# The two latent projections as one group of eight half-bank tiles, with x in five pieces

## The chip, the cores and the metric

The kernel runs on one core of a Trainium2 chip. The metric is the device time of one execution, in microseconds (us). The engines are TensorE (PE: matmuls, turned tiles), ScalarE (ACT), VectorE (DVE), GpSimd (POOL) and SyncE (SP, which issues most transfers); each runs its own instructions in order and waits for the others at semaphores.

## The reference, cut to what matters

A block of 256 tokens of width 2048 goes through two layers. The change touches only the start of the first: the normed x times the first 1024 columns of `w_in`, which are the query latent `q_a` and the key and value latent `c_kv`, 512 columns each, and what reads them.

```python
h = _rmsnorm(x, pre_norm_g)
proj = jnp.einsum('bsd,de->bse', h, w_in)
(q_a, c_kv, k_rope, z_mla, ...) = jnp.split(proj, cuts, axis=-1)
q = jnp.einsum('bsr,re->bse', _rmsnorm(q_a, q_a_norm_g), w_q_b)
kv = jnp.einsum('bsr,re->bse', _rmsnorm(c_kv, kv_a_norm_g), w_kv_b)
```

## The kernel before

**Units.** Every weight matrix is cut into units of 128 x 1024 fp32 values (512 KB). A unit is loaded by SP into one of four slots (`w_raw`), rounded by ACT into `w_hi`, and the rest `w_raw - w_hi` is made by DVE as `w_lo`, both in one of three slots. In this text the two halves of the split of unit i together are called W(i). A projection product is three matmuls: hi by hi, hi by the operand's lo, lo by hi. The helper `run` goes through a phase's units; before unit i it makes sure that splits up to i + 2 are in the plan, and after it adds split i + 3. So ACT's half of W(i + 3) waits until PE has used unit i. `plan_work` writes one list of steps, and each engine takes its part of every step in that order; nothing else sets the order.

**The start.** ACT issues the identity and x (four pieces of 512 KB, `first_loads`); SP issues the first unit, the constants, three more units and some small rows. x comes with tokens on the partitions. `x_tile(k)` turns one tile of 128 columns of both token halves: two transposes on PE into one of three side banks, a copy to SBUF on DVE (`x_T`, L1881), gain and rounding on ACT (`op_hi`, L1576), a square on ACT (L1581), and the square's sum on POOL (L2393). The lo half of tile k - 1 (`op_lo`, L1886) follows on DVE. Six tiles are turned ahead of the first unit and ten later, one in two PE tiles.

**The latents.** Phases `qa` and `kva` each hold one group of four tiles of 128 output columns, over 16 tiles of x: 8 units of 2 x 512, a unit being 24 matmuls. Call the 16 units of both u0 to u15. Phase `kr` (2 units, u16 and u17, of 24 matmuls each) and phase `q` (16 units of 18 matmuls) follow. When a group is done, DVE multiplies each tile by the factor R of the first norm (`latent`, L1976), ACT squares it (L1609), POOL adds, and 4 PE tiles later `latent_split` makes the operand's halves: ACT (L1616), DVE (L1990).

**Factors.** A norm's factor is made by `row_sum` (PE sums the squares, DVE L1897, POOL's power, DVE L1903) and `row_spread` (PE), then copied by DVE (L1911). `factor` jobs, and the job `vectors`, stand in `pending`, and `pump` runs one step of each active job after a unit. `vectors` turns the small rows (`cols`, after u6), converts the positions (`pos_f`, DVE L1917), multiplies them out on PE (`angle`, after u7, which waits for `pos_f`), and makes the sines in DVE steps (L1923 to L1952). R is `r1`, the latent factors are `rq` and `rkv`.

Of the kernel before, what the change touches and what calls it, by code (L numbers as in the profile page):

```python
# [12 lines left out]
ALU = mybir.AluOpType  # L13
# [12 lines left out]
H1, DN, RD, DV, LORA = 16, 128, 64, 128, 512  # L26
C_QA, C_KV, C_KR = 0, LORA, 2 * LORA
# [181 lines left out]
FOUR, THREE, ONE = ("f0", "f1", "f2", "f3"), ("f0", "f1", "f2"), ("f0",)  # L209
KV = ("f0", "f2", "t0", "t1")  # L210
TOKENS = ("t0", "t1")


def groups_of(c0, n, cols=512, tiles=FOUR):
    return [(c0 + g * cols, cols, tiles) for g in range(n)]


def phases():
    ph = {}

    def put(name, *args, **kw):
        ph[name] = Phase(name, *args, **kw)

    put("qa", "w_in", groups_of(C_QA, 1), KT, "h", S)
    put("kva", "w_in", groups_of(C_KV, 1), KT, "h", S)
    put("kr", "w_in", [(C_KR, P, ONE)], KT, "h", S)
# [40 lines left out]
def plan_work(sem):  # L267
# [39 lines left out]
    def later(step, tiles=4):  # L307
        deferred.append([tiles, step])
# [10 lines left out]
    def run(p, evac):  # L319
        out = {}  # L320
        for i in range(p.first, p.end):
            split_to(i + LEAD)
            u = units[i]
            for m, tile in enumerate(u.tiles):
                if u.k0 == 0:
                    out[m] = banks.take()
                last = m == len(u.tiles) - 1
                s = add("tile", i, m, bank=out[m], marks="proj" if u.last else "used" if last else "")
                if last:
                    plan.used[i] = s["proj" if u.last else "used"]  # L330
                for d in deferred:
                    d[0] -= 1
                for d in [d for d in deferred if d[0] <= 0]:
                    deferred.remove(d)
                    d[1]()
                if u.last:
                    out[m].ends(evac(u.g, m, out[m].slot, s["proj"]))
            if not (p.hold and i == p.end - 1):
                split_to(i + N_SPLIT)
            if (i - p.first) % p.period == p.period - 1:  # L340
                pump()
# [41 lines left out]

    add("first_loads", dma="ld_ident ld_x0 ld_x1 ld_x2 ld_x3")
    zero = add("zero_rows", marks="rows_zero")["rows_zero"]
    pre = add("load_pre", dma="ld_pre", zero=zero)["ld_pre"]
    load()
    done["con"] = add("load_con", dma="ld_con")["ld_con"]
    for _ in range(N_RAW - 1):
        load()  # L390
# [25 lines left out]
    for k in range(KT):  # L416
        if k < 6:
            x_tile(k)
        else:
            later(lambda k=k: x_tile(k), 2 * (k - 5))  # L420
        if k in (2, 4):
            split()
# [42 lines left out]

    def latent(which):
        def evac(g, m, pb, got):
            sc = scratch.take() if m else None
            s = add("latent", which, m, marks="evac sq" + (" sq_acc" if m else ""), pb=pb, got=got, scratch=sc)
            if m:  # L470
                sc.ends(s["sq_acc"])

            def split_latent():
                done["lat_" + which, m] = add("latent_split", which, m, marks="op_hi op_lo", x=s["evac"])["op_lo"]
            later(split_latent)
            if m == 3:
                pending.append(factor("r" + which, [s["sq_acc"]], delay=4))
            return s["evac"]
        return evac

# [90 lines left out]

    run(ph["qa"], latent("q"))
    run(ph["kva"], latent("kv"))
    run(ph["kr"], evac_kr)
    flush()
# [439 lines left out]
class Memory:  # L1015
# [221 lines left out]
def tensor_engine(nc, m, plan, S_):  # L1237
# [16 lines left out]
    def tile(s):  # L1254
# [10 lines left out]
        for k in range(u.nk):  # L1265
            kt = u.k0 + k
            operand_ready(u.phase.operand, kt)
            x_hi, x_lo = m.operand(u.phase.operand, kt)
            first, last = kt == 0, kt == u.phase.ktiles - 1
            if kind == "f":  # L1270
# [25 lines left out]
    def x_tile(s):  # L1296
        k, = s.args
        bank = s.of["bank"]
        pe.wait_ge(S_("ld_ident"), 16)
        pe.wait_ge(S_(f"ld_x{k // 4}"), 16)  # L1300
        pe.wait_ge(*bank.after)
        b = m.side[bank.slot]
        turn(b[:, 0:P], m.x_in[:, 0, COLS(k)], ident)
        turn(b[:, P:S], m.x_in[:, 1, COLS(k)], ident).then_inc(S_("xt_t"), 1)
# [246 lines left out]
def scalar_engine(nc, m, a, plan, S_):  # L1551
# [301 lines left out]
def vector_engine(nc, m, plan, S_):  # L1853
# [707 lines left out]
```

## Time and profile before

| | us |
|---|---|
| median of 3 runs | 2036.23 |
| lowest, highest | 2033.36, 2036.35 |
| the profiled execution | 2034.77 |
| its span | 2033.5 |

The 1.3 us between the profiled time and its span lie outside the instructions. The profiled execution is 1.5 us under the median. Times in the rows are us from the start of the span, the second number being the duration, and a bracket at the end says how long the engine was idle before and who released it.

### The profile page before, as it was taken

How to read it: one execution, taken by the hardware profiler on the slowest of the kernel's cores; microseconds unless marked ns; L12 is line 12 of the kernel's file. 1: busy time of each engine (PE TensorE's matmuls, PEld its weight loads, DVE VectorE, ACT ScalarE, POOL GpSimd, SP SyncE). 2: the span in 40 equal slices, each digit the busy share in tenths (PEclk: the TensorE clock that was granted, in tenths of full speed). 3: DMA queues.
4: the chain of work that ended last, by engine and by line, in shares of the span. 5: the costliest groups of instructions: out<-in, count | busy, mean ns of one | idle time of the engine just before them, and what ended most of it. 6: DMA issues, size and time to landing. Idle time of an engine off the chain costs nothing.

```text
span 2033.5 us, 37130 instructions
## 1 busy us (share of the span) xinstructions
PE 1978.8 (97%) x15778; PEld 1941.9 (95%) x15778; DVE 1169.5 (58%) x1736; ACT 875.5 (43%) x1264; POOL 298.9 (15%) x336
## 2 busy tenths in 40 slices
PE   7999999999999999999999799999999998999999
PEld 6999999999999999999999699999999998999987
DVE  5765665555554545644554655576467676564654
ACT  5444454434444434444444433445443333344443
POOL 2110010202010003300211521030011122030200
PEclk9999999999999999999999899999999999999999
DMA  7466555556666565565565364443564443556564
GB/s 241 138 193 173 152 154 157 156 177 183 182 185 181 184 186 176 180 192 182 185 221 182 126 192 137 145 136 113 157 177 135 125 125 115 177 180 192 186 226 158
DMA packets 177695, 343.79 MB, mean 169 GB/s; under 512 B 10478, under 2 KB 19050, under 8 KB 177002
## 3 DMA queue, kind: packets, MB, share of 16 engines
q1 hardware_dynamic: 176154, 337.16, 54.8%
q10 hardware_dynamic: 1376, 4.26, 0.6%
q8 instruction: 124, 2.03, 0.4%
q14 instruction: 41, 0.34, 0.0%
HBM read 335.09 MB, written 6.29 MB: 168 GB/s over the span
## 4 chain that ended last, share of the span: by engine, by line
PE 82%; issue 8%; DVE 3%; POOL 2%; ACT 1%; POOLq 0%; DVEq 0%; ACTq 0%
PE bank L1245 81%; DVE w_lo L1866 1%; POOL arena L2467 1%; ACT w_hi L1567 1%; POOL scratch L2464 1%; DVE arena L2146 0%; POOL arena L2511 0%; POOL stats L2413 0%; DVE head_factor L1903 0%; DVE arena L2249 0%; DVE best L2247 0%; ACT scratch L1725 0%; DVE ob_lo L2151 0%; ACT ob_hi L1723 0%; POOL acc_a L2393 0%
## 5 line engine op out<-in xcount | busy, mean ns | idle before, releaser
L1866 DVE TENSOR_TENSOR w_lo<-w_raw,w_hi 128x1024 fp32r<-128x1024 f32 (+2 forms) x644 | 784.9, 1222 | 786.4 <-ACT w_hi L1567 785.1
L1567 ACT ACTIVATE w_hi<-w_raw 128x1024 fp32r<-128x1024 f32 (+2 forms) x644 | 661.5, 1031 | 925.0 <-PE bank L1245 924.5
L1245 PE MATMUL bank<-hb_hi,w_hi 128*128 128x256 f32 x2448 | 700.3, 286 | 0.1
L1245 PE MATMUL bank<-hb_lo,w_hi 128*128 128x256 f32 x2448 | 694.1, 284 | 0.0
L1245 PE MATMUL bank<-hb_hi,w_lo 128*128 128x256 f32 x2448 | 694.1, 284 | 0.0
L1245 PE MATMUL bank<-ob_hi,w_hi 128*128 128x256 f32 (+1 forms) x2224 | 650.9, 293 | 9.1 <-DVE ob_lo L2151 6.6
L1245 PE MATMUL bank<-ob_hi,w_lo 128*128 128x256 f32 (+1 forms) x2224 | 631.7, 284 | 0.0
L1245 PE MATMUL bank<-ob_lo,w_hi 128*128 128x256 f32 (+1 forms) x2224 | 630.5, 284 | 0.0
L1245 PEld LDWEIGHTS bank<-hb_hi,w_hi 128*128 128x128 f32 x2448 | 470.4, 192 | 2.4 <-DVE w_lo L1866 1.3
L1245 PEld LDWEIGHTS bank<-hb_lo,w_hi 128*128 128x128 f32 x2448 | 470.5, 192 | 0.4
L1245 PEld LDWEIGHTS bank<-hb_hi,w_lo 128*128 128x128 f32 x2448 | 470.5, 192 | 0.0
L1245 PEld LDWEIGHTS bank<-ob_hi,w_hi 128*128 128x128 f32 x2224 | 424.8, 191 | 13.8 <-issue 4.4
L1245 PEld LDWEIGHTS bank<-ob_lo,w_hi 128*128 128x128 f32 x2224 | 424.7, 191 | 1.5
L1245 PEld LDWEIGHTS bank<-ob_hi,w_lo 128*128 128x128 f32 x2224 | 424.0, 191 | 0.0
L1245 PE MATMUL bank<-arena 128*128 128x64 f32 (+4 forms) x618 | 102.6, 303 | 10.4 <-DVE arena L2333 3.0
L1245 PEld LDWEIGHTS bank<-arena 128*128 128x128 f32 x618 | 80.6, 191 | 14.0 <-DVE arena L2333 3.3
L2474 POOL TENSOR_TENSOR arena<-scratch,arena 128x256 f32<-128x256 f32 x32 | 31.9, 1030 | 278.7 <-DVE scratch L1976 278.7
L1245 PE MATMUL bank<-w_hi,ob_hi 128*128 128x512 f32 (+1 forms) x192 | 69.0, 359 | 0.0
L1245 PE MATMUL bank<-w_lo,ob_hi 128*128 128x512 f32 (+1 forms) x192 | 68.5, 357 | 0.0
L1245 PE MATMUL bank<-w_hi,ob_lo 128*128 128x512 f32 (+1 forms) x192 | 68.4, 356 | 0.0
L2447 POOL TENSOR_TENSOR arena<-arena,factor 128x256 f32<-128x256 f32 x16 | 15.3, 990 | 276.5 <-DVE arena L1976 276.5
L2464 POOL TENSOR_TENSOR scratch<-scratch,head_factor 128x256 f32<-128x256 f32 x16 | 13.3, 833 | 242.9 <-ACT head_factor L1680 242.9
(252 smaller groups left out, 1227.4 us busy)
## 6 DMA issues: line engine op xcount, KB each, us to landing
w_raw<-in_w_in SPq DMA_DIRECT2D x436, 512.0 KB, 3.7
w_raw<-in_w_out SPq DMA_DIRECT2D x64, 512.0 KB, 4.1
w_raw<-in_w_o_conv SPq DMA_DIRECT2D x32, 512.0 KB, 4.4
w_raw<-in_w_o_mla SPq DMA_DIRECT2D x32, 512.0 KB, 3.8
w_raw<-in_w_branch SPq DMA_DIRECT2D x32, 512.0 KB, 4.0
w_raw<-in_w_kv_b SPq DMA_DIRECT2D x16, 512.0 KB, 3.9
w_raw<-in_w_q_b SPq DMA_DIRECT2D x16, 384.0 KB, 3.2
arena<-x_kept SPq DMA_DIRECT2D x2, 2048.0 KB, 9.1
```

Of the source, the lines that this page charges most:

```text
L1245: return nc.tensor.matmul(dst, lhsT, rhs, start=start, stop=stop, skip_group_check=True)
L1567: act(dst, src, ACT.Copy).then_inc(S_("w_hi"), 1)
L1866: tt(low, src, high.bitcast(F32), ALU.subtract).then_inc(S_("w_lo"), 1)
L2447: tt(m.u_t[:, t, :], m.u_t[:, t, :], m.R, ALU.mult).then_inc(S_("conv_b"), 1)
L2464: tt(z, z, ring[s.of["head"].slot][:, 0:S], ALU.mult).then_inc(S_("silu"), 1)
L2467: tt(y, z, y, ALU.mult).then_inc(S_("gated"), 1)
L2474: tt(y, m.scratch[s.of["scratch"].slot][:, 0:S], y, ALU.add).then_inc(S_("merged"), 1)
```

## The change

Phases `qa` and `kva` become one phase `lat` with a group of eight tiles over 1024 columns. A unit is then one tile of x by 1024 columns, 4 KB rows where they were 2 KB, and still 24 matmuls; there are still 16. Two tiles share a PSUM bank: the odd one starts without the start flag and is placed in the upper 256 columns, and both are read out after the odd one's last matmul. x comes as 2, 2, 4, 4 and 4 tiles. SP issues a second unit ahead of the constants. Four tiles are turned ahead of the first unit and twelve later, one in six PE tiles. The latent splits come 2 tiles after their read-out, not 4, and the job `rq` waits 2 pumps, not 4.

```diff
-    put("qa", "w_in", groups_of(C_QA, 1), KT, "h", S)
-    put("kva", "w_in", groups_of(C_KV, 1), KT, "h", S)
+    put("lat", "w_in", groups_of(C_QA, 1, 2 * LORA, EIGHT), KT, "h", S)
...
-        out = {}
+        out, two = {}, len(p.groups[0][2]) > 4
...
-                    out[m] = banks.take()
+                    out[m] = out[m - 1] if two and m % 2 else banks.take()
...
-                if u.last:
+                if u.last and not two:
+                    out[m].ends(evac(u.g, m, out[m].slot, s["proj"]))
+                elif u.last and m % 2:
+                    evac(u.g, m - 1, out[m].slot, s["proj"])
                     out[m].ends(evac(u.g, m, out[m].slot, s["proj"]))
...
-    add("first_loads", dma="ld_ident ld_x0 ld_x1 ld_x2 ld_x3")
+    add("first_loads", dma="ld_ident ld_x0 ld_x1 ld_x2 ld_x3 ld_x4")
...
     load()
+    load()
     done["con"] = add("load_con", dma="ld_con")["ld_con"]
-    for _ in range(N_RAW - 1):
+    for _ in range(N_RAW - 2):
         load()
...
-        if k < 6:
+        if k < 4:
             x_tile(k)
         else:
-            later(lambda k=k: x_tile(k), 2 * (k - 5))
-        if k in (2, 4):
+            later(lambda k=k: x_tile(k), 6 * (k - 3))
+        if k in (0, 2):
             split()
...
+        later(split_latent, 2)
+        if m == 3:
+            pending.append(factor("r" + which, [s["sq_acc"]], delay=2 if which == "q" else 4))
...
-    run(ph["qa"], latent("q"))
-    run(ph["kva"], latent("kv"))
+    run(ph["lat"], latent)
...
+X_PARTS = ((0, 2), (2, 4), (4, 8), (8, 12), (12, 16))
...
+        if len(u.tiles) > 4:
+            return self.proj[bank][:, S * (m % 2):S * (m % 2) + S]
...
-            first, last = kt == 0, kt == u.phase.ktiles - 1
+            first, last = kt == 0 and not (len(u.tiles) > 4 and t % 2), kt == u.phase.ktiles - 1
```

**Order, place A.** DVE around the conversion of the positions (`small`, the CAST), between u6 and u8. In the kernel before, where no turned tile is left:

```order
L1866 TENSOR_TENSOR w_lo<-w_raw,w_hi 128x1024 [waits w_hi] x2
L1897 TENSOR_SCALAR stats0<-bank7 128x2 [waits rf_sum]
L1903 TENSOR_SCALAR acc_b<-con,stats0 128x128 [waits rf_pow]
L1903 TENSOR_SCALAR acc_b<-con,stats0 128x128
L1866 TENSOR_TENSOR w_lo<-w_raw,w_hi 128x1024 [waits w_hi]
L1915 COPY cols<-bank5 128x112 [waits cols_t]
L1917 CAST small<-arena 1x256 [waits ld_pos]
```

and in the changed kernel, whose line numbers are 5 higher here, from W(8) on:

```order
L1871 TENSOR_TENSOR w_lo<-w_raw,w_hi 128x1024 [waits w_hi]
L1886 COPY arena<-bank6 128x256 [waits xt_t]
L1891 SCALAR_TENSOR_TENSOR hb_lo<-arena,cols,hb_hi 128x256 [waits op_hi]
L1871 TENSOR_TENSOR w_lo<-w_raw,w_hi 128x1024 [waits w_hi]
L1920 COPY cols<-bank7 128x112 [waits cols_t]
L1922 CAST small<-arena 1x256 [waits ld_pos]
L1886 COPY arena<-bank5 128x256 [waits xt_t]
L1891 SCALAR_TENSOR_TENSOR hb_lo<-arena,cols,hb_hi 128x256 [waits op_hi]
```

The CAST stands right behind W(9) in both, but now turned tile 12 and eleven others have gone through DVE and ACT between the splits ahead of it, and the work on R comes after it.

**Order, place B.** PE at the end of u7, the kernel before:

```order
L1245 MATMUL bank3<-hb_hi,w_hi 128x256
L1245 MATMUL bank3<-hb_lo,w_hi 128x256
L1245 MATMUL bank3<-hb_hi,w_lo 128x256
L1245 MATMUL bank7<-small,con 128x256 [waits rf_mean,pos_f]
L1245 MATMUL bank4<-hb_hi,w_hi 128x256 [waits w_lo]
```

and the changed kernel:

```order
L1250 MATMUL bank3<-hb_hi,w_hi 128x256
L1250 MATMUL bank3<-hb_lo,w_hi 128x256
L1250 MATMUL bank3<-hb_hi,w_lo 128x256
L1250 MATMUL bank6<-small,con 128x256 [waits x_T,pos_f]
L1250 MATMUL bank0<-hb_hi,w_hi 128x256 [waits op_lo,w_lo]
```

The matmul on `small` (`angle`) keeps its place behind u7 and its wait for the CAST of place A.

**Order, place C.** DVE at the end of the latents (L1976, now L1992: the read-out; L1990, now L1998: the split's lo half). Before:

```order
L1866 TENSOR_TENSOR w_lo<-w_raw,w_hi 128x1024 [waits w_hi]
L1957 TENSOR_TENSOR small2<-cols 128x8 [waits cols]
L1959 TENSOR_TENSOR small2<-cols,small2 128x8 [waits dve_own]
L1960 TENSOR_TENSOR small2<-cols,small2 128x8
L1976 TENSOR_TENSOR arena<-bank4,factor 128x256 [waits proj]
L1976 TENSOR_TENSOR arena<-bank0,factor 128x256 [waits proj]
L1976 TENSOR_TENSOR arena<-bank1,factor 128x256 [waits proj]
L1976 TENSOR_TENSOR arena<-bank2,factor 128x256 [waits proj]
L1866 TENSOR_TENSOR w_lo<-w_raw,w_hi 128x2x256 [waits w_hi]
```

and now:

```order
L1992 TENSOR_TENSOR arena<-bank0,factor 128x256 [waits rf_out,proj]
L1992 TENSOR_TENSOR arena<-bank0,factor 128x256
L1998 SCALAR_TENSOR_TENSOR ob_lo<-arena,cols,ob_hi 128x256 [waits op_hi] x2
L1992 TENSOR_TENSOR arena<-bank1,factor 128x256 [waits proj]
L1992 TENSOR_TENSOR arena<-bank1,factor 128x256
L1998 SCALAR_TENSOR_TENSOR ob_lo<-arena,cols,ob_hi 128x256 [waits op_hi] x2
L1992 TENSOR_TENSOR arena<-bank2,factor 128x256 [waits proj]
L1992 TENSOR_TENSOR arena<-bank2,factor 128x256
L1998 SCALAR_TENSOR_TENSOR ob_lo<-arena,cols,ob_hi 128x256 [waits op_hi] x2
L1992 TENSOR_TENSOR arena<-bank3,factor 128x256 [waits proj]
L1992 TENSOR_TENSOR arena<-bank3,factor 128x256
L1871 TENSOR_TENSOR w_lo<-w_raw,w_hi 128x2x256 [waits w_hi]
```

The first split of phase `q`, W(18), stood behind four read-outs and now stands behind eight, with three pairs of latent splits between them. From the second unit of the third query group on, the instructions of every engine stand as before.

## Rows read from the trace of the kernel before

**Rows 1.** The page: busy time by engine, share of the span, instructions.
```profile
PE 1978.8 (97%) x15778; PEld 1941.9 (95%) x15778; DVE 1169.5 (58%) x1736; ACT 875.5 (43%) x1264; POOL 298.9 (15%) x336
```

**Rows 2.** Waits of PE, 0 to 110 us: total, times, longest in us.
```profile
PE bank L1303 <- DMA arena<-in_x: 5.8, 2, 3.0
PE bank L1245 <- POOL acc_b L2393: 3.5, 1, 3.5
...
PE bank L1245 <- DVE acc_b L1903: 1.4, 1, 1.4
...
PE bank L1245 <- DVE acc_a L1903: 1.2, 1, 1.2
```

**Rows 3.** Timeline, PE's first projection matmul: start, duration, engine, line, tiles.
```profile
11.92 0.58 PE L1245 MATMUL bank<-hb_hi,w_hi 128*128 128x256 f32 x1
```

**Rows 4.** The load tile w_raw, issues at 2.4 and 3.2 us: time until landed.
```profile
L1185 SPq DMA_DIRECT2D w_raw<-in_w_in x2: 542/656/769, 2.4 to 3.2; - x2
...
DMA to landing us min/median/max: 10.5/11.5/12.5
```

**Rows 5.** Timeline of ACT, 13 to 34 us: the w_hi halves of four units.
```profile
13.68 1.04 ACT L1567 ACTIVATE w_hi<-w_raw 128x1024 fp32r<-128x1024 f32 x1
...
17.07 1.05 ACT L1567 ACTIVATE w_hi<-w_raw 128x1024 fp32r<-128x1024 f32 x1
...
29.48 1.04 ACT L1567 ACTIVATE w_hi<-w_raw 128x1024 fp32r<-128x1024 f32 x1
...
33.59 1.05 ACT L1567 ACTIVATE w_hi<-w_raw 128x1024 fp32r<-128x1024 f32 x1
```

**Rows 6.** Timeline of DVE, 30 to 34 us: the w_lo half of a unit.
```profile
30.55 1.23 DVE L1866 TENSOR_TENSOR w_lo<-w_raw,w_hi 128x1024 fp32r<-128x1024 f32 x1 [1.44 <-ACT w_hi L1567]
```

**Rows 7.** Stretches: busy us and records by engine, granted clock, DMA share, GB/s.
```profile
41.00:43.00 2.00, 2.00 (x12) 2.00 (x11) 0.70 (x4) 0.00 (x0) 0.71 (x1) 0.50 0.93 393
43.00:45.00 2.00, 2.00 (x14) 2.00 (x14) 0.03 (x1) 1.06 (x1) 0.00 (x0) 0.71 0.90 300
120.00:150.00 30.00, 30.00 (x254) 29.94 (x253) 17.96 (x26) 14.44 (x19) 2.22 (x3) 1.00 0.65 191
1129.00:1143.00 14.00, 7.90 (x35) 7.29 (x35) 11.12 (x17) 5.32 (x13) 10.86 (x13) 0.52 0.15 61
```

**Rows 8.** Timeline of all engines, 62 to 65 us: the factor of the query latent.
```profile
62.66 0.15 DVE L1897 TENSOR_SCALAR stats<-bank 128x2 f32<-128x2 f32 x1
...
64.26 0.68 PE L1245 MATMUL bank<-acc_a,con 128*128 128x128 f32 x4 [1.17 <-DVE acc_a L1903]
```

**Rows 9.** Timeline of DVE, 45 to 100 us.
```profile
46.30 0.27 DVE L1917 CAST small<-arena 1x256 f32<-1x256 int32 x1
...
51.40 1.76 DVE L1990 SCALAR_TENSOR_TENSOR ob_lo<-arena,cols,ob_hi 128x256 fp32r<-128x256 f32 x4
...
65.43 0.42 DVE L1939 SCALAR_TENSOR_TENSOR rope<-scratch 128x256 f32<-128x256 f32 x1
...
66.68 0.42 DVE L1911 COPY factor<-bank 128x256 f32<-128x256 f32 x1
...
73.70 1.41 DVE L1976 TENSOR_TENSOR arena<-bank,factor 128x256 f32<-128x256 f32 x4
...
81.31 1.01 DVE L1866 TENSOR_TENSOR w_lo<-w_raw,w_hi 128x512 fp32r<-128x512 f32 x2
```

**Rows 10.** Timeline of ACT, 45 to 100 us.
```profile
49.73 1.69 ACT L1616 ACTIVATE ob_hi<-arena,cols 128x256 fp32r<-128x256 f32 x4
...
71.13 1.04 ACT L1567 ACTIVATE w_hi<-w_raw 128x1024 fp32r<-128x1024 f32 x1
```

**Rows 11.** Timeline of PE: the angle matmul, the meta turns, the rope of query group 0.
```profile
47.39 0.69 PE L1245 MATMUL bank<-small,con 1*128 1x256 f32 x2
...
79.27 1.17 PE L1352 MATMUL bank<-con,arena 16*128 16x16 f32 x16
...
94.97 0.59 PE L1245 MATMUL bank<-arena,con 128*128 128x256 f32 x2
```

More of the change, by code:

```diff
@@ L210 @@
 KV = ("f0", "f2", "t0", "t1")
+EIGHT = tuple(f"f{j}" for j in range(8))
 TOKENS = ("t0", "t1")
@@ L462, in plan_work, with latent, split_latent @@
     pending.append(vectors())
[L466 to L479, printed above, removed]
+    def latent(g, n, pb, got):
+        which, m = ("q", "kv")[n // 4], n % 4
+        sc = scratch.take() if m else None
+        s = add("latent", which, m, marks="evac sq" + (" sq_acc" if m else ""), pb=pb, got=got, scratch=sc)
+        if m:
+            sc.ends(s["sq_acc"])
+        def split_latent():
+            done["lat_" + which, m] = add("latent_split", which, m, marks="op_hi op_lo", x=s["evac"])["op_lo"]
+        later(split_latent, 2)
+        if m == 3:
+            pending.append(factor("r" + which, [s["sq_acc"]], delay=2 if which == "q" else 4))
+        return s["evac"]
     def clear_halves(kind, free):
@@ L1299, in x_tile @@
         pe.wait_ge(S_("ld_ident"), 16)
-        pe.wait_ge(S_(f"ld_x{k // 4}"), 16)
+        pe.wait_ge(S_(f"ld_x{[k < hi for lo, hi in X_PARTS].index(True)}"), 16)
         pe.wait_ge(*bank.after)
@@ L1556, in first_loads @@
         nc.scalar.dma_start(m.con[:, 0:P], a["const_f"][:, 0:P]).then_inc(S_("ld_ident"), 16)
-        for j in range(4):
-            x = a["x"][0, :, j * 512:(j + 1) * 512].rearrange("(b p) n -> p b n", p=P)
-            nc.scalar.dma_start(m.x_in[:, :, j * 512:(j + 1) * 512], x).then_inc(S_(f"ld_x{j}"), 16)
+        for j, (lo, hi) in enumerate(X_PARTS):
+            x = a["x"][0, :, lo * P:hi * P].rearrange("(b p) n -> p b n", p=P)
+            nc.scalar.dma_start(m.x_in[:, :, lo * P:hi * P], x).then_inc(S_(f"ld_x{j}"), 16)
     def split(s):
@@ L1983, in latent @@
         which, t = s.args
-        out_by(s, m.LAT[:, 4 * (which == "kv") + t, :], m.R, done["r1"])
+        at = S * (t % 2)
+        ve.wait_ge(*s.of["got"])
+        ve.wait_ge(*done["r1"])
+        tt(m.LAT[:, 4 * (which == "kv") + t, :], m.proj[s.of["pb"]][:, at:at + S], m.R, ALU.mult).then_inc(S_("evac"), 1)
     def latent_split(s):
```

## The prediction

> **What bounds the kernel now.** I read the page first: PE is busy 97% of the span [rows 1], so only PE's idle time and its clock can be won or lost. Then PE's waits up to 110 us [rows 2]: 5.8 us for x to land, one wait of 3.5 for the sum of x's squares (`acc_b`) and one of 1.2 and one of 1.4 for a latent's factor. The reader is to see that these are few and single, and that the matmuls begin at 11.92 [rows 3]. Then the laps of ACT and DVE [rows 5, 6], because the splits W(i) and the turned tiles hand each other on between these two: ACT's half of a split, DVE's half 1.07 us behind it (30.55 less 29.48), DVE's copy of a turned tile, ACT's rounding and square of it, ACT's next half. With one turned tile between two splits a lap is 17.07 - 13.68 = 3.39 us, with two 33.59 - 29.48 = 4.11. PE's unit takes 24 x 0.118 = 2.83 (30.00 us by 254 records [rows 7]) and 0.2 per turned tile. In this stretch ACT and DVE bound the kernel, not PE. Last the clock: after the wait of 3.5 us the granted clock is 0.50, the 1.2 GHz level, from 41 to 43 and 0.71 on average from 43 to 45 [rows 7], which costs 1.0 + 0.6 = 1.6 us of matmul time.
>
> **The start.** W(0) no longer waits for turned tiles 1 and 2, and x's first two tiles come as 256 KB. DVE's half of W(0) should end about 1 us before 11.92. I cost it at nothing, because what comes below is set by the laps and not by PE: even from 11.92, eight units with the slow clock at the beginning (8 x 2.83, some 2.5, my estimate, for the slow matmuls, 10 turned tiles at 0.2) bring PE to the end of u7 at 39.1 or so.
>
> **Place A and B, the wait for `pos_f`.** PE's `angle` behind u7 waits for the CAST behind W(9). W(2) can't start before its load has landed. It is the third unit issued in both kernels, behind the same bytes: 3.2 + 12.5 = 15.7 [rows 4]. From W(2) to W(9) there are seven laps, five with one turned tile (4, 5, 8, 9, 12) and two with two (6 and 7, 10 and 11): 5 x 3.39 + 2 x 4.11 = 25.2. So ACT's half of W(9) starts at 41.0, DVE's at 42.0, and with its 1.23 [rows 6] and the copy and CAST of 0.27 each [rows 9] `pos_f` is there at 43.7. PE waits there from about 39.3: a new wait of 4.4 us. Queued behind it on PE are u8, whose W(8) is ready at 39.9, and everything else. In the kernel before `angle` ran at 47.39 [rows 11], so PE passes this point 3.6 us earlier than before, but with work left that it had then done: turned tiles 14 and 15 (0.4), the row sum and the row spread of `r1` (1.0). Lead: 3.6 - 1.4 = 2.2.
>
> The load's price has a second value. The rows of a load are now 4 KB and not 2. The Trainium skill, page "DMA: Bandwidth & Descriptors", section "Why small descriptors are slow (HBM only)", states about 3 cycles per packet beside one per 32 bytes; as an estimate from that page, 67 against 65.5 cycles per 2 KB, W(2) would land 0.3 us earlier and the sum would be 0.3 less. No row here shows a 4 KB load.
>
> **The clock behind that wait.** The wait of 3.5 cost 1.6 in slow matmuls [rows 2, 7]; this one is longer, so I take the same 1.6. Lead: 0.6. Bounds: 0, if the engine's idle time falls otherwise than before, and 3.2, two such stretches.
>
> **The wait for R.** The row sum of `r1` stood behind u5, its spread behind u6, and only two splits stood ahead of it on DVE. Now the sum comes after u9 and the spread after u10, and DVE has ahead of it, from the end of u9: ACT's and DVE's halves of W(12), which wait for u9 (1.07 + 1.15), the three sine steps L1939 to L1943 (66.68 - 65.43 = 1.25 [rows 9]) and then 64.26 - 62.66 = 1.6 from DVE's first step of a factor to PE's spread [rows 8]. That is 5.1, against u10 and the row sum, 3.3: a wait of 1.8 to 2.0. I take 2.0, since W(12) also queues behind two steps of `turns`. The 3.5 us wait for `acc_b` goes: between turned tile 15 and the sum lies all of u9. Its saving is already in the 3.6 above. Lead: 0.6 - 2.0 = -1.4, a lag.
>
> **The factor of the query latent.** `rq`'s sum (0.5), wait (1.2 [rows 2]) and spread (0.5) stood between u11 and u13 and now stand behind `kr`. So u15 ends 2.2 - 1.4 = 0.8 us earlier than before.
>
> **Place C, the read-out.** Before, half of the latents was read out in the middle, under `kva`. Now all eight come behind u15. DVE's first read-out follows ACT's half of W(17) by 73.70 - 71.13 = 2.57 [rows 9, 10]; that half starts when u14 is used, which is u15 and `kr` (3 x 2.83) ahead of 79.27, 70.7, and 69.8 now. So the read-out starts at 72.4. A pair is a lap of its own: two read-outs (1.41 / 4 = 0.35 each [rows 9]), two squares on ACT as long, two hi halves (1.69 / 4 = 0.42 [rows 10]), the second lo half (1.76 / 4 = 0.44 [rows 9]). The pair after it waits for that: 0.7 + 0.35 + 0.85 + 0.44 and the handing over, 2.4 us. Three laps bring the last pair to 79.6. Its squares end at 80.7; behind them ACT and DVE do W(18), two pieces, 1.7 us (DVE's two take 1.01 [rows 9], ACT's first lies ahead of them). W(18) is ready at 82.4. PE has done `kr` and the meta turns at 79.6 (79.27 + 1.17 [rows 11], 0.8 earlier) and the row sum of `rq` at 80.1. A wait of 2.3, where there was none.
>
> Then the spread of `rq`, one unit of 2.1 later. DVE has ahead of it W(19) 0.95, the bounds' small steps 0.6, two lo halves 0.9, two memsets 0.6, `kr`'s read-out 0.3, W(20) 0.95, and 1.6 as above: 5.9. A wait of 3.7. Of these the 0.6 and 0.6 are estimates from neighbouring short rows; bounds of the whole are 2.5 and 4.5. The wait for `rkv` falls from 1.4 [rows 2] to about 0.4, since the splits wait less when PE is late.
>
> Up to the rope of query group 0's successor at 94.97 [rows 11], behind which every engine's order is as before: -0.8 + 1.0 (sum and spread of `rq`) + 2.3 + 3.7 + 0.4 - 1.4 = +5.2 us.
>
> **The clock behind those waits.** PE then stands idle for 6 of 8.2 us. The nearest case is 1129 to 1143, where the clock was 0.52 on average over 14 us with PE busy 7.9 [rows 7], which cost up to 3.9. Here one stretch costs 1.6 and a run as there 3.9; I take 1.9, nearer to the first, as the idle time is shorter. Sum: +5.2 + 1.9 = +7.1 us.
>
> The sum stands on the profiled execution, 2034.8, and gives 2041.9 there. The profiled execution is 1.5 under the median, and nothing in the change touches that distance: 2036.2 + 7.1 = 2043.3.
>
> **The rivals.**
> Late waits hidden: the 8 us of `kr`, meta turns and row sum cover the read-out laps, if a pair takes under 1.4 us because ACT and DVE work at two pairs at once. For it: ACT and DVE are only half busy over the span [rows 1]. Against it: both run in order and the order has the lo halves of a pair ahead of the next read-out. It takes away 2.3 + 3.7 + 1.9 and leaves the `rkv` wait at 1.4: 2043.3 - 6.9 = 2036.4. Chance 0.14.
> Early wait missing: `pos_f` comes before PE is through with u7, and only the late waits hold. PE then goes on at W(8) and W(9), u9 starts at 43.4 and not at 48.5 (43.8, u8 with two turned tiles 3.2, slow clock 1.6): 2043.3 - 5.1 = 2038.2. It would take W(2) landed 4 us earlier. Chance 0.11.
> The other side: handing over between ACT and DVE gets cheap when less is turned per unit. Its place is both laps; it decides where a lap with one turned tile falls to PE's own 3.0 us and a pair of read-outs to 1.4. Both cases above then hold together: 2043.3 - 6.9 - 5.1 = 2031.3, faster. Against it stands the lap of 3.39 that the trace has with just one turned tile [rows 5]. Chance 0.12.
> A further 3 us of slow clock at the three waits, to 2047 or so, is within the forecast.
>
> **How the numbers follow.** A measurement of this kernel can tell about 0.2% from no change, 4.1 us: faster is under 2032.2, slower over 2040.3. The forecast with its bounds spans 2040.3 to 2049 and has a chance of 0.63. The two middle rivals are within 0.2%: 0.25. The other side is 0.12. A range from 2034.5 to 2049 leaves out the other side and some 0.05 of the tails.
>
> **What would show it.** In the profile of the changed kernel: PE's first projection matmul near 10.8; a PE wait of about 4.4 us for DVE's CAST ending near 43.7, with the granted clock at 0.50 behind it; a PE wait of about 2 for `acc_b` on DVE near 57, and none on POOL; DVE's read-outs in four pairs, 2.4 us apart, from 72.4; PE waits of 2.3 for `w_lo` and 3.7 for `acc_a` between 80 and 89. The forecast is wrong if the first is under 1 us, which would mean that the laps are not what holds W(9), or if the pairs of read-outs stand closer than 1.5 us.

## The result, and the profile after

The changed kernel takes 2042.2 us (median of 6 runs, 2041.2 to 2043.4) against 2035.7 for the kernel before beside it: a ratio of 1.0035, 95% interval 1.0023 to 1.0046. A second batch of the same kernel gave 2043.1 and 1.0037 (1.0025 to 1.0050). It is slower, within the range and 1.1 us under the forecast of 2043.3. The profiled execution took 2042.17, its span 2040.9. The agreement hides an error in one term of the forecast, the slow clock, which the second half of this section takes apart.

The busy row answers to [rows 1]:

```profile
PE 1977.9 (97%) x15778; PEld 1940.0 (95%) x15778; DVE 1170.1 (57%) x1736; ACT 875.8 (43%) x1264; POOL 299.0 (15%) x336
```

PE's share is the same 97%, with 0.9 us less busy time in a span that is 7.4 longer. Its waits from 0 to 110 us answer to [rows 2] (total, times, longest):

```profile
PE bank L1250 <- DVE w_lo L1871: 4.6, 2, 4.2
...
PE bank L1250 <- DVE small L1922: 4.0, 1, 4.0
...
PE bank L1250 <- DVE acc_b L1908: 2.6, 2, 1.9
PE bank L1250 <- DVE acc_a L1908: 1.9, 1, 1.9
```

POOL's 3.5 for `acc_b` is gone and four waits stand in its place. The timeline of PE shows where each of them ends (start, duration, then in brackets the idle time and who ended it); the first row answers to [rows 3] and the last, the rope of query group 0's successor, to 94.97 in [rows 11]:

```profile
10.76 0.55 PE L1250 MATMUL bank<-hb_hi,w_hi 128*128 128x256 f32 x1 [0.96 <-DVE hb_lo L1891]
...
43.09 1.22 PE L1250 MATMUL bank<-small,con 1*128 1x256 f32 x2 [4.02 <-DVE small L1922]
...
57.60 0.68 PE L1250 MATMUL bank<-acc_b,con 128*128 128x128 f32 x4 [1.89 <-DVE acc_b L1908]
...
85.77 0.58 PE L1250 MATMUL bank<-ob_hi,w_hi 128*128 128x256 f32 x1 [4.22 <-DVE w_lo L1871]
...
91.51 0.68 PE L1250 MATMUL bank<-acc_a,con 128*128 128x128 f32 x4 [1.88 <-DVE acc_a L1908]
...
105.32 0.59 PE L1250 MATMUL bank<-arena,con 128*128 128x256 f32 x2
```

They are 4.0, 1.9, 4.2 and 1.9 us, and a fifth of 0.7 ends at 102.65. The last row stands 10.35 us behind the kernel before. I call this point Z. From here on all engines run the same instructions in the same order in both kernels. DVE's side of the four waits, which answers to [rows 6, 9]:

```profile
41.44 1.23 DVE L1871 TENSOR_TENSOR w_lo<-w_raw,w_hi 128x1024 fp32r<-128x1024 f32 x1 [1.44 <-ACT w_hi L1572]
...
42.76 0.27 DVE L1922 CAST small<-arena 1x256 f32<-1x256 int32 x1
...
54.74 0.42 DVE L1944 SCALAR_TENSOR_TENSOR rope<-scratch 128x256 f32<-128x256 f32 x1
...
74.28 0.75 DVE L1992 TENSOR_TENSOR arena<-bank,factor 128x256 f32<-128x256 f32 x2
...
76.91 0.74 DVE L1992 TENSOR_TENSOR arena<-bank,factor 128x256 f32<-128x256 f32 x2
...
79.81 0.74 DVE L1992 TENSOR_TENSOR arena<-bank,factor 128x256 f32<-128x256 f32 x2
...
82.41 0.74 DVE L1992 TENSOR_TENSOR arena<-bank,factor 128x256 f32<-128x256 f32 x2
84.15 2.16 DVE L1871 TENSOR_TENSOR w_lo<-w_raw,w_hi 128x512 fp32r<-128x512 f32 x3 [1.00 <-ACT w_hi L1572]
```

W(9) and, right behind it, the CAST; the three sine steps from 54.74 ahead of r1's diag; the read-outs in pairs 2.6, 2.9 and 2.6 us apart, and W(18) only then. The stretches of TensorE's clock (columns as in [rows 7]: busy time of PE, its weight loads, DVE, ACT, POOL, then the granted clock):

```profile
13.00:95.00 82.00, 69.19 (x514) 67.07 (x513) 51.85 (x107) 39.72 (x72) 16.15 (x21) 0.88 0.52 166
41.30:48.10 6.80, 5.01 (x20) 4.36 (x21) 4.67 (x9) 2.68 (x6) 0.76 (x2) 0.50 0.42 133
58.40:61.80 3.40, 3.40 (x18) 3.40 (x18) 0.72 (x3) 0.42 (x1) 0.00 (x0) 0.50 0.98 283
82.30:89.10 6.80, 3.33 (x15) 3.34 (x16) 5.53 (x17) 4.29 (x11) 1.94 (x2) 0.50 0.33 101
92.50:95.90 3.40, 3.40 (x16) 3.22 (x15) 2.27 (x6) 0.00 (x0) 0.00 (x0) 0.50 0.39 128
```

Before Z the clock is at 0.50, the 1.2 GHz level, in four stretches, 20.4 us together, where the kernel before has one of 3.4 (40.8 to 44.2). As an estimate I count half of PE's busy time in such a stretch as lost: (5.01 + 3.40 + 3.33 + 3.40) / 2 = 7.6 us, against 1.7.

**What becomes of the 10.35.** I matched DVE's arithmetic instructions of the two traces one by one from the end. The lag stays between 10.35 and 10.56 up to 1601 us (times as in the kernel before), is 9.07 at 1605, stays near 9 up to 1684, is 7.41 at 1688 and stays there. Set side by side, the same two time spans of before and of after show what the falls are (columns as above):

```profile
1600.00:1605.00 5.00, 5.00 (x32) 5.00 (x31) 1.94 (x4) 0.57 (x1) 0.00 (x0) 0.66 0.58 187
1682.00:1687.00 5.00, 5.00 (x31) 5.00 (x32) 2.88 (x6) 0.00 (x1) 0.00 (x0) 0.66 0.33 108
```

```profile
1600.00:1605.00 5.00, 5.00 (x45) 5.00 (x44) 4.21 (x10) 1.06 (x1) 0.74 (x1) 1.00 0.48 132
1682.00:1687.00 5.00, 5.00 (x45) 5.00 (x44) 3.79 (x6) 1.06 (x1) 0.85 (x1) 1.00 0.30 105
```

The execution of before has a half-clock stretch of 3.4 us in each, where the mean falls to 0.66; that of after has none. (A third, at 1631 in before, costs nothing, since the lag is 9.05 on both sides of it.) In the second batch of the changed kernel, with the same instructions, they are back:

```profile
1607.00:1612.00 5.00, 5.00 (x32) 5.00 (x31) 1.78 (x4) 0.73 (x1) 0.00 (x0) 0.66 0.53 175
1689.00:1694.00 5.00, 5.00 (x33) 5.00 (x31) 2.72 (x6) 0.17 (x1) 0.00 (x0) 0.66 0.34 108
```

There the lag is 7.93 at Z, its start having been 1.15 us earlier, and 6.85 at the end, with no step at these two places. So each profiled execution holds a few stretches of slow clock by chance, and about 3 of the 10.35 came back by such a chance. The two steps, 1.5 and 1.7 us, also say how good the estimate by halves is: it gives 1.7 for each, and 1.7 for the third, which cost nothing. It's an upper one.

### The profile page after: what moved, and what is told of

The parts are those of the page before. It is cut to its first block, busy times and chain, and to the rows that moved or that the text cites. A ratio compares the mean times of both kernels' runs of the same rounds, so it can differ in the third digit from the quotient of the medians.

```text
span 2040.9 us, 37138 instructions
## 1 busy us (share of the span) xinstructions
PE 1977.9 (97%) x15778; PEld 1940.0 (95%) x15778; DVE 1170.1 (57%) x1736; ACT 875.8 (43%) x1264; POOL 299.0 (15%) x336
## 4 chain that ended last, share of the span: by engine, by line
PE 82%; issue 9%; DVE 5%; ACT 2%; POOL 2%; DMA 0%; ACTq 0%; POOLq 0%; DVEq 0%
PE bank L1250 81%; DVE w_lo L1871 2%; ACT w_hi L1572 1%; POOL arena L2475 1%; POOL scratch L2472 1%; DVE arena L2154 0%; POOL stats L2421 0%; POOL arena L2519 0%; ACT scratch L1586 0%; DMA arena<-in_x 0%; DVE ob_lo L1998 0%; DVE head_factor L1908 0%; DVE arena L1886 0%; DVE arena L2257 0%; ACT hb_hi L1581 0%
```

## The experiments

To read all of them in one way I split the time up to Z into three parts: the start of the first projection matmul; PE's idle time behind it (the sum of its waits of over 0.2 us); and half of PE's busy time in half-clock stretches, as an estimate of what the clock took. Where the three are subtracted from those of before, Z follows within 1.4 us, mostly within 0.6. Batches compare each kernel with the kernel before on the same chip (medians 2035.2 to 2035.7). The ratio isn't the quotient of the two medians: in the batch of experiments 1 to 4, for one, 7 of 30 runs of the kernel before took only 2029 to 2030.4 us. The four columns up to Z are those of one profiled execution, which isn't always a typical one: it took 2037.8 in experiment 1 and 2040.3 in 6, 2.2 and 4.1 under the median, and 2037.5 in 7, 3.8 over it; in the others it lies within 1.6.

| kernel | first matmul | idle | clock | Z | median | ratio (95%) |
|---|---|---|---|---|---|---|
| before | 11.92 | 7.3 | 1.7 | 94.97 | 2035.7 | |
| changed | 10.76 | 13.5 | 7.6 | 105.32 | 2042.2 | 1.0035 (1.0023 to 1.0046) |
| changed, again | 9.61 | 13.0 | 6.4 | 102.90 | 2043.1 | 1.0037 (1.0025 to 1.0050) |
| 1 CAST early | 9.66 | 13.2 | 1.8 | 99.00 | 2040.0 | 1.0028 (1.0017 to 1.0039) |
| 2 r1 first | 10.15 | 12.0 | 6.5 | 102.47 | 2041.2 | 1.0036 (1.0023 to 1.0048) |
| 3 read-outs in a row | 10.54 | 9.3 | 5.6 | 99.22 | 2038.6 | 1.0024 (1.0013 to 1.0034) |
| 4 all three | 9.70 | 5.6 | 4.6 | 94.68 | 2032.3 | 0.9992 (0.9982 to 1.0002) |
| 5 start alone | 9.61 | 8.1 | 3.2 | 94.87 | 2034.6 | 0.9993 (0.9984 to 1.0002) |
| 6 grouping alone | 12.73 | 13.2 | 5.3 | 104.88 | 2044.4 | 1.0039 (1.0027 to 1.0051) |
| 7 five edits | 11.26 | 7.5 | 5.0 | 97.76 | 2033.7 | 0.9993 (0.9983 to 1.0002) |
| 8 tiles 8 apart | 9.78 | 8.2 | 3.4 | 95.84 | 2035.1 | 0.9999 (0.9990 to 1.0008) |
| 9 later row sum | 10.38 | 7.9 | 1.7 | 95.21 | 2034.0 | 0.9994 (0.9985 to 1.0003) |
| 10 both | 11.29 | 7.6 | 1.6 | 95.90 | 2033.7 | 0.9991 (0.9982 to 1.0000) |
| 11 later spread | 11.23 | 6.1 | 0 | 92.15 | 2029.0 | 0.9973 (0.9963 to 0.9982) |

**Experiment 1: the CAST early.**

```diff
     def vectors():
+        done["pos_f"] = add("pos_cast", marks="pos_f")["pos_f"]
         for _ in range(5):
             yield
...
-        s = add("cols", marks="cols_t cols pos_f", bank=b)
+        s = add("cols", marks="cols_t cols", bank=b)
...
+
+    def pos_cast(s):
         ve.wait_ge(*done["pos"])
         v.tensor_copy(m.pos_f, m.pos_i).then_inc(S_("pos_f"), 1)
```

> Edit: DVE's CAST of the positions (pos_f) stands behind W(1) instead of behind W(9), nothing else. My theory (laps of ACT and DVE): the early PE wait of 4.0 us at 39 to 43 goes, because PE's angle step no longer waits for W(9). But the laps themselves don't get faster: W(9) is still ready at 42.6, W(10) near 46, W(11) near 50, then W(12) and the three sine steps, so DVE's diag of r1 comes near 54.7 and not 57.4, and PE, there since about 49.5, waits for it 4.5 to 5.5 us instead of 1.9. Of the 4.0 only 2.8 are kept: 2042.2 - 2.8 = 2039.4 us, between 2037.5 and 2041 with one half-clock stretch of 1.7 more or less. Rival in the record (the early wait missing is worth 5.1): 2037.1. Rival that the order of DVE has nothing to do with it, and PE waits for splits anyway: the wait at 39 stays over 3 us under w_lo's name and the time at 2042.

Measured: 2040.0, near the expected 2039.4. The CAST runs at 23.06, directly behind W(4) and not behind W(1) as I had it; that is still 15.8 us ahead of its use. The timeline of PE:

```profile
38.84 0.67 PE L1251 MATMUL bank<-small,con 1*128 1x256 f32 x2 [0.69 <-DVE arena L1887]
...
41.99 0.33 PE L1309 MATMUL bank<-con,arena 128*128 128x128 f32 x1 [1.58 <-DVE cols L1921]
...
48.78 0.58 PE L1251 MATMUL bank<-con,acc_b 128*128 128x1 f32 x4 [1.11 <-POOL acc_b L2404]
...
54.34 0.68 PE L1251 MATMUL bank<-acc_b,con 128*128 128x128 f32 x4 [2.01 <-DVE acc_b L1909]
```

The 4.0 us wait for the CAST has become 0.7 at the same `angle` matmul, so DVE's order is its cause. R's spread comes at 54.34 (54.7 expected), so the laps held back most of what was won. The size of that I had right and the shape wrong: the remaining idle time is not one wait of 5 us but three single ones, of 1.6 for the copy of `cols` (behind W(9) on DVE as the CAST was, and it holds the bank of the next turned tile), 1.1 and 2.0. Idle time thus fell by only 0.4. What fell in this execution is the clock's part, 7.6 to 1.8; the runs of this kernel go from 2034.5 to 2042.5, so that isn't shown for a typical one.

**Experiment 2: r1's first steps ahead of the sine steps.**

```diff
-            pending.appendleft(factor("r1", [done["x_sq"]], delay=1))
+            active.insert(0, factor("r1", [done["x_sq"]], delay=1))
```

> Edit: DVE's first two steps of r1's factor (mean, diag) stand ahead of the three sine steps instead of behind them, nothing else. My theory: the wait of 1.9 us for R's spread at 55.7 shrinks by the 1.25 us of the three sine steps to 0.6 or 0.7, the other waits stay (4.0 early, 4.2 + 1.9 + 0.7 late). 2042.2 - 1.2 = 2041.0 us; 2039.3 if the half-clock stretch of 58.4 to 61.8 behind that wait goes too (its cost is 3.4 / 2 = 1.7). Rival (the wait is made by W(12), which needs u9, and not by the sine steps): the wait stays at 1.9 and the time at 2042.2.

```profile
56.27 0.68 PE L1250 MATMUL bank<-acc_b,con 128*128 128x128 f32 x4 [0.63 <-DVE acc_b L1908]
```

The wait is 0.63 and not 1.89: the three sine steps of DVE are its cause, as the prediction had it, and the half-clock stretch at 58.4 is gone too. No new wait has come, and Z comes 2.85 us earlier. Of that 0.6 is an earlier start. The median is 1.0 under that of the changed kernel (1.9 under its second batch), but the two intervals overlap nearly wholly: the wait is shown, a gain in time is not.

**Experiment 3: the read-outs in a row.**

```diff
-        later(split_latent, 2)
+        later(split_latent, 8)
```

> Edit: the splits of the latents are put off by 8 tiles instead of 2, so the eight read-outs on DVE and the eight squares on ACT stand in a row, then W(18) and W(19), then the hi and lo halves of the latents. My theory (pairs hand over between ACT and DVE and hold W(18) back): read-outs 0.35 apart from 74.3 to 77.1, W(18) ready near 79.5 instead of 85.6, so PE's wait of 4.2 for w_lo goes, and that of 1.9 for acc_a falls to 0.5 to 1: 6.8 becomes about 1.2. With it go the half-clock stretches at 82.3 to 89.1 and 92.5 to 95.9 in part (5.1 us if both went, half of that taken). 2042.2 - 5.6 - 2.5 = 2034.1 us, between 2031.5 and 2037. Early waits stay 4.0 and 1.9. Rival (the wait there is the price of eight tiles at once and not of their order): w_lo's wait stays above 3 us and the time at 2041 to 2042.

Timeline of DVE, then of PE:

```profile
74.00 2.74 DVE L1992 TENSOR_TENSOR arena<-bank,factor 128x256 f32<-128x256 f32 x8
...
82.46 0.55 PE L1250 MATMUL bank<-ob_hi,w_hi 128*128 128x256 f32 x1 [1.20 <-DVE ob_lo L1998]
```

The eight read-outs take 2.74 us in a row, and PE's wait for W(18) is gone; it now waits 1.2 for a latent's lo half, and the one of 1.9 for `acc_a` is gone. The late waits are 2.5 and not 6.8 (1.2 expected). So the order of the pairs makes most of the late waits, and not the number of eight tiles. The time is 2038.6, short of 2034.1 by 1.3 in idle time and by the clock, of which only 2.0 came back, and by stretches behind Z.

**Experiment 4: the three together.** The diff is that of the three.

> Edit: the three edits together (CAST behind W(1), r1's first steps ahead of the sine steps, the latents' splits put off by 8 tiles). My theory: the wait for the CAST gone, the wait for R's spread ending near 53.5 instead of 57.6 (2.8 + 1.2 = 4.0 us kept), the late waits about 1.2 instead of 6.8 (5.6), clock 2.5: 2042.2 - 4.0 - 5.6 - 2.5 = 2030.1 us, between 2027 and 2033, so faster than the kernel before (2035.7) as well. Rival (the grouping costs what it costs, whatever the order): not below 2038.

Measured: 2032.3, inside the expected range; Z is 10.6 us earlier than in the changed kernel. Singly the three edits took 2.2, 1.0 and 3.6 us off the median, together 9.9, which is more than their sum; in idle time it is 0.4, 1.6 and 4.3 against 7.9. The loss of the change is thus made by three places in the order and not by the half banks or the 4 KB loads, which this version keeps; its ratio (0.9992) is that of the start alone with two groups (0.9993, experiment 5). Against the kernel before, the interval reaches to 1.0002, so it isn't shown to be faster. This kernel and that of experiment 1 have the same two waits, 0.7 and 1.6, between 38 and 43 us. The same stretch of each, first experiment 1, then experiment 4:

```profile
38.00:49.00 11.00, 7.62 (x59) 6.80 (x57) 7.31 (x15) 6.44 (x12) 3.00 (x4) 1.00 0.55 176
```

```profile
38.00:49.00 11.00, 8.74 (x47) 8.04 (x46) 7.09 (x14) 5.86 (x11) 2.84 (x4) 0.69 0.54 173
```

In one of them the clock stays at 1.00, in the other it falls, for 6.8 us from 41.1 on. Waits of this size don't set the clock by themselves.

**Experiments 5 and 6: the two halves of the change alone.** The start on the kernel before (two groups stay):

```diff
-        if k < 6:
+        if k < 4:
             x_tile(k)
         else:
-            later(lambda k=k: x_tile(k), 2 * (k - 5))
-        if k in (2, 4):
+            later(lambda k=k: x_tile(k), max(k - 3, 2 * (k - 5)))
+        if k in (0, 2):
```

> The kernel before with the start of the change alone: x in five pieces, w_raw's second load ahead of con's, four tiles turned ahead and W(0) and W(1) behind turned tiles 0 and 2; two groups of four tiles stay, and turned tile 15 stays where it is in the kernel before (20 tiles in), since R has to be there for the first read-out behind u7. My theory: the first projection matmul comes near 10.8 instead of 11.9, W(2) starts near 16.2 instead of 17.1, and the wait for acc_b behind turned tile 15 stays at 3 to 3.5 us, so the start gives back 0.9 to 1.1 us and no wait is added: 2035.2 - 1.0 = 2034.2 us, between 2033 and 2036. Rival (the start carries part of the loss, through the loads or through fewer tiles ahead): over 2037.

and the grouping with the start of before:

```diff
-        if k < 4:
+        if k < 6:
             x_tile(k)
         else:
-            later(lambda k=k: x_tile(k), 6 * (k - 3))
-        if k in (0, 2):
+            later(lambda k=k: x_tile(k), 6 * (k - 5))
+        if k in (2, 4):
```

> The changed kernel with the grouping alone: eight tiles of one group two to a bank, but x in four pieces, con's load behind the first w_raw load, six tiles turned ahead, the rest six tiles of the projection apart (turned tile 15 at 60 tiles, 12 earlier). My theory: W(2) starts at 17.1, so W(9) and the CAST end 0.9 to 1.8 us later (44 to 45) and PE waits there 4 to 5 us; R's factor is 1.5 units earlier, ahead of the sine steps, and its wait of 1.9 falls under 0.7, perhaps with its half-clock stretch (1.7); the late waits stay 4.2 + 1.9 + 0.7. Changed kernel 2042.2 + 1.4 - 1.7 - 0.8 = 2041.1 us, between 2039.5 and 2043: the whole loss comes with the grouping. Rival (the loss comes from the start, not from the grouping): 2035 to 2037.

The start alone: 2034.6, as expected a small gain or none (its interval holds 1). The first matmul comes 2.3 us earlier and Z only 0.1: a new wait of 1.5 for a turned tile, and 1.5 more of the clock around the same 3.47 for `acc_b`. The grouping alone: 2044.4 (5 runs, 2040.3 to 2045.5), the whole loss and more. I missed by 3.3; the profiled execution was one of the two at 2040.3, so its rows explain a part only: the first matmul came at 12.73, and R's wait fell only to 1.5, since its diag on DVE, now ahead of the sine steps, still stands behind W(11), which waits for u8 and so for PE's own wait for the CAST. So the three places of experiment 4 come with the grouping, which puts the read-outs of eight tiles behind one unit and the turned tiles between the splits for longer.

**Experiments 7 to 11: is there a version that beats both?** Seven has the edits of four, `cols` in the middle of a unit and the latents' splits after 7 tiles; eight has turned tiles 8 apart as well. Nine is seven with r1's row sum one unit later and the latents' splits after 8 tiles again, ten is the same with turned tiles 8 apart.

```diff
+        later(cols, 4)
...
-        later(split_latent, 8)
+        later(split_latent, 7)
```

> The three edits of before together, and two more: DVE's copy of cols stands in the middle of a unit, ahead of a split and not behind W(9), and the latents' splits are put off by 7 tiles, so that those of the first pair stand ahead of W(19). Three-edit version 2032.3. My theory: the wait of 1.6 at 40.4 for cols goes, but what follows is bound by the laps to W(11) and W(12), so R's spread still ends near 54 and at most 0.3 us are kept in idle time; the late wait of 1.2 for a latent's lo half falls to about 0.5. 2032.3 - 1.0 = 2031.3 us, and 2028 if the half-clock stretch of 41.1 to 47.9 (6.8 us, 3.4 lost at most) is gone as well; between 2027.5 and 2032. Rival (each PE wait counts by itself): 2032.3 - 1.6 - 0.7 = 2030.0 without the clock, with R's spread near 52.7.

```diff
-            later(lambda k=k: x_tile(k), 6 * (k - 3))
+            later(lambda k=k: x_tile(k), 8 * (k - 3))
...
-        b, ang, turns = side.take(), scratch.take(), scratch.take()
+        b, ang, turns = side.take(), heads.take(), heads.take()
```

> As the version with five edits, and the turned tiles stand 8 tiles of the projection apart and not 6, one to each unit (the angle's buffers are two head_factor tiles instead of two scratch tiles, so that the longer row of turned tiles doesn't run into them). My theory: every lap of ACT and DVE then has one turned tile and takes 3.39 us, none takes 4.11; W(i) starts at 16.2 + 3.39 x (i - 2), so W(15) at 60.3, and PE waits some 0.3 us at each unit but not over 1 us in a row up to u15; R's factor stands behind turned tile 15 and meets no wait over 1 us. u15 ends near 64.5 to 66 instead of 69.4. 2032.3 - 4 = 2028 us, between 2024.5 and 2031. Rival (the laps aren't what binds up to 60 us, PE's own work and clock are): no gain over the five-edit version, 2030 or more, and single waits of over 1.5 us stay.

Both missed: 2033.7 and 2035.1, no gain on experiment 4. The runs of seven fall into two groups, six from 2029.5 to 2032.1 with a mean granted clock of 0.992 to 0.993 and six from 2035.4 to 2037.5 with 0.988 to 0.990; the profiled one is the slowest. A wait that is new in it:

```profile
50.37 0.98 PE L1255 MATMUL bank<-con,acc_b 128*128 128x1 f32 x4 [2.86 <-POOL acc_b L2408]
```

With the early waits gone PE runs ahead of the laps and reaches r1's row sum before the last square is added: 2.9 us in seven and 3.8 in eight, where experiment 4 had none of that name. Neither of my expectations for seven had that: the 1.6 for `cols` and the 0.6 for the spread went and this one of 2.9 came, and at the end the latents' splits after 7 tiles made a wait of 2.6 for `acc_a` where experiment 4 had one of 1.2 and I had expected 0.5. In eight the rival held, in the time and in this, that a single wait of over 1.5 us stayed; the waits at single units were under 0.6, as the laps' theory had it.

```diff
-            active.insert(0, factor("r1", [done["x_sq"]], delay=1))
+            active.insert(0, factor("r1", [done["x_sq"]], delay=2))
```

> The five-edit version with r1's row sum one unit later (behind u10, its spread behind u11; R isn't needed before the read-outs behind u15) and the latents' splits put off by 8 tiles again. The trace of the five-edit version shows a single PE wait of 2.9 us for acc_b on POOL, which follows the laps. My theory: that wait falls to under 0.5, W(11) or the spread takes at most 1 us of it, and the late wait for acc_a of 2.6 is again one of 1.2 for a lo half. Against the three-edit version (2032.3), whose waits of 1.6 for cols and 0.6 for the spread go, and 1 us for W(11) comes: idle time 1.2 to 2.2 less, one or no half-clock stretch less (1.7): 2032.3 - 2.5 = 2029.8 us, between 2027.5 and 2032. Rival (the idle time only moves once more to the next thing that the laps make late): 2032 or more.

> The same with turned tiles 8 tiles of the projection apart, one to each unit (row sum of r1 behind u13, spread behind u14). The trace of the first such version shows laps short enough (PE's waits at single units 0.3 to 0.6 us) and a single wait of 3.8 us for acc_b, since turned tile 15 comes at 96 tiles and the row sum right behind the next unit. My theory: with the sum one unit later that wait falls under 1, and with it the half-clock stretch of 58.8 to 62.3 behind it (1.7); the late wait of 2.4 is 1.2 again. 2035.1 - 3.0 - 1.7 - 1.2 = 2029.2 us, between 2026.5 and 2032. Rival (the idle time moves on): 2033 or more.

2034.0 and 2033.7, over their ranges by 2.0 and 1.7. The wait for `acc_b` is gone, and the spread behind it waits 2.4 us for its diag. The rival (the idle time moves on) held in both. A unit of 2.8 us between sum and spread is less than ACT, DVE and POOL need for the split ahead of it and the diag. That names the next edit:

```diff
-        b, t = yield from row_factor(what, squares, head=head)
+        b, t = yield from row_factor(what, squares, wait=2 if what == "r1" else 1, head=head)
```

with the bounds' four steps moved behind the meta turn.

> The version with the later row sum (2034.0), and two more moves: the spread of r1 stands two units behind its row sum instead of one, and the bounds' four short steps on DVE stand behind the meta turn and not ahead of the first latents' lo halves. The trace of that version shows single PE waits of 2.4 us for the spread of r1 and of 1.2 and 1.3 for a lo half and for rq's diag. My theory (a wait is gone when what it waits for stands one unit of work ahead of it): the 2.4 falls under 0.3 with the half-clock stretch behind it (1.7), the 1.2 + 1.3 by some 0.6. 2034.0 - 2.3 - 1.7 - 0.6 = 2029.4 us if the clock stretch goes, 2031.1 if it comes elsewhere; between 2028.5 and 2033. Rival (idle time only moves to the next thing): 2033.5 or more, with a new single wait of over 1.5 us before 77.

Measured: 2029.0, ratio 0.9973 (0.9963 to 0.9982), 0.3% faster than the kernel before and 0.6% than the changed one. Its waits from 13 to 110 us, and the stretch 13 to 95 that answers to the first row of the clock above:

```profile
PE bank L1258 <- DVE ob_lo L2008: 1.5, 1, 1.5
PE bank L1258 <- DVE acc_b L1916: 1.4, 1, 1.4
PE bank L1258 <- DVE acc_a L1916: 1.4, 1, 1.4
PE bank L1316 <- DVE arena L1894: 1.3, 1, 1.3
PE bank L1258 <- DVE w_lo L1879: 0.6, 1, 0.6
```

```profile
13.00:95.00 82.00, 75.84 (x612) 73.89 (x611) 60.24 (x127) 43.04 (x82) 19.38 (x26) 1.00 0.59 182
```

No wait is over 1.5 us. The clock is 1.00 on average where the changed kernel has 0.88, and PE is busy 75.8 us of the 82 and not 69.2. The 2.4 for the spread is gone and the time is near that expected with the clock's stretch gone (2029.4). In part that is luck: Z comes only 3.1 us earlier than in nine and 2.8 earlier than in the kernel before, while the medians differ by 5.0 and 6.3. Matched as above, this execution gains a further 1.8 on that of before at 1175 us, where the order is the same. That this version is faster is shown; that its order before Z earns all of it isn't. The late waits are 4.3 together where nine had 3.8, and I had expected 0.6 less: moving the bounds brought nothing.

**Experiment 12: the changed kernel again.**

> The changed kernel once more, unchanged, to see what of its clock belongs to the program and what to the run. If the half-clock stretches beyond 1100 us fall where the program puts them, the trace has again about 20 us of them at 1140 to 1185 and none from 1550 to 1720, and the time is 2042.2. If they fall by the run, the trace has single stretches of 3.4 us between 1550 and 1720 as most other kernels of this study have, each costing 1.5 to 1.7, and the medians of two batches may differ by one or two of them, up to 2045. The waits before 110 us should be the same within 0.1 us in either case.

The waits are the same within 0.2 us (4.01, 1.89, 4.22, 1.69, 0.75). The stretches beyond 1100 us are not: three single ones between 1600 and 1700, as shown above. So at least these fall by the run.

## Why the prediction was right, and where it was not

**The three waits: right, with their causes.** The CAST: 4.4 forecast, 4.0 measured, ending at 43.1 and not 43.7; experiment 1 shows the cause. R: 2.0 forecast, 1.9 measured; experiment 2. The late ones: 2.3 + 3.7 + 0.4 = 6.4 forecast, 4.2 + 1.9 + 0.7 = 6.8 measured; experiment 3. The share between the first two of these was off: the pairs took 2.7 us on average and not 2.4, began at 74.3 and not 72.4, and W(18) and W(19) followed each other directly, so more of the work that I had put behind the row sum lay ahead of it.

**"I cost it at nothing": the start, wrong.** The step said that what comes below is set by the laps and not by PE, and put their beginning, W(2), at the landing of its load at 15.7. So an earlier W(0) could change nothing. But the load landed earlier (query of tile `w_raw`, the third issue, answering to [rows 4]; first the changed kernel, then experiment 5, with the same order of loads but 2 KB rows):

```profile
L1190 SPq DMA_DIRECT2D w_raw<-in_w_in x1: 580/580/580, 2.9 to 2.9; - x1
...
DMA to landing us min/median/max: 9.6/9.6/9.6
```

```profile
L1187 SPq DMA_DIRECT2D w_raw<-in_w_in x1: 716/716/716, 3.0 to 3.0; - x1
...
DMA to landing us min/median/max: 10.8/10.8/10.8
```

Landing was at 2.9 + 9.6 = 12.5, and W(2) was held by the laps from W(0) on, 4.11 and then 3.40 after it (timeline of ACT, answering to [rows 5]):

```profile
7.59 1.04 ACT L1572 ACTIVATE w_hi<-w_raw 128x1024 fp32r<-128x1024 f32 x1
...
11.70 1.04 ACT L1572 ACTIVATE w_hi<-w_raw 128x1024 fp32r<-128x1024 f32 x1
...
15.10 1.04 ACT L1572 ACTIVATE w_hi<-w_raw 128x1024 fp32r<-128x1024 f32 x1
```

Everything behind moves with W(0): in the second batch W(1) and W(2) start at 10.56 and 13.95, 1.15 us earlier, and so does the first matmul (9.61) and the end of the wait for the CAST (41.94). In the first batch's profile the error is small: W(2) started 0.7 us earlier than I had it (1.8 in the second batch). I had also used the Trainium skill, page "DMA: Bandwidth & Descriptors", section "Why small descriptors are slow (HBM only)", for an estimate that 4 KB rows bring W(2) 0.3 us forward. The rows show 1.2 between experiment 5 and the changed kernel, where the x loads beside them are the same, and 1.4 against the second batch (9.4). With the order of loads of before it is 10.6 in experiment 6 with 4 KB rows and 12.5 in the kernel before with 2 KB [rows 4]. So both pairs show more than the estimate; these are single executions, and why isn't tested. The page speaks of the packets themselves and not of a queue with others in it.

**"A further 3 us of slow clock": the term that was mis-sized.** I took 1.6 behind the first wait and 1.9 behind the late ones, 3.5 together, and none behind R's. In the profiled execution they took 2.5, 1.7 and 3.4, which is 7.6, and 6.4 in the second batch. That makes up the distance between the forecast and what was measured at Z: 7.1 + 4.1, less 0.6 since the CAST ended that much earlier, and 0.3 more for the waits behind it (8.7 against 8.4), is 10.9 against 10.35. The 0.5 too much may lie in counting half of the busy time, which is an upper estimate. The end of the profiled execution agreed with 7.1 (it lags by 7.4) since about 3 us came back at 1600 and 1685, by chance as experiment 12 shows. The medians, over more runs, put the loss at 6.5 and 7.8. So the waits were forecast rightly, and that the total came out within 1.1 us is in part luck. Of that 1.1, 0.5 is the base: over six runs the kernel before has a median of 2035.7 and not 2036.2.

**The rivals.** "Late waits hidden" and "the other side" had ACT and DVE work faster than their laps; the pairs took longer than forecast, not less. "Early wait missing" needed W(2) 4 us earlier; it started 0.7 earlier. Its price of 5.1 was wrong: experiment 1 takes the wait away and R's spread comes only 3.3 us earlier, of which 1.1 is the start of that run, because the laps to W(12) stay. I had priced the removal of a wait by the wait itself, and not by what is late next.

**Still open.** Why the clock fell behind some single waits of 1.2 to 2.4 us and not behind others isn't settled. Nor is how many of the stretches beyond 1100 us a typical execution has, so no median can be worked out from one profile to better than some 3 us. The shorter delay of the job `rq`, a part of the change, was never run by itself.

## What to carry to other kernels

Where two engines hand a unit back and forth, measure the lap from one start to the next and follow it back to the first: everything hung behind a unit in the in-order queue (a CAST of 0.27 us here) costs PE a lap when it is needed. Place it ahead of that unit, and put one more unit between a reduction and its use than its chain takes. Price the removal of a wait by what is ready next behind it: versions 7 to 10 moved idle time from one wait to the next, and the one in which no wait was over 1.5 us was faster than before.

## What the runs showed of the hardware

- The half-clock stretches before Z came 3.4, 6.8 or 10.2 us long, and some began while PE was still idle (at 41.3, in a wait from 39.1 to 43.1). All waits of 3.5 us and more behind the first projection matmul had one behind or in them; of the waits of 1.9 to 2.0 for R's spread three (changed, again, experiment 3) had one and one (experiment 1) had none; of the four of 1.2 for a latent's lo half three (experiments 3, 4 and 10) had one and one (experiment 9) had none; the three of 1.4 to 1.5 in experiment 11 had none. So the length of the wait alone doesn't tell. The Trainium skill, page "TensorE: Matmul & The Clock Gate", Part 1, says that the same kernel varies from run to run in its slow matmuls at the start; these traces show the same of stretches in the middle (experiment 12 against the changed kernel).
- The first projection matmul of the same kernel came at 10.76 and at 9.61, a difference of 1.15 us in the start that went through to Z.
